# First block's rows by a one-hot product, counts in three products and block stores on ScalarE's DMA queue, in the experts of two layers

## What is computed

```python
def moe(x, router_w, router_b, w_gate, w_up, w_down):
    scores = sigmoid(xf @ router_w)
    biased = scores + router_b
    # best group by its two best, then the two best experts of that group
    _, idx = lax.top_k(jnp.where(in_group, biased, -jnp.inf), TOP_K)
    w = take_along_axis(scores, idx); w = w / sum(w)
    counts = jnp.bincount(idx.reshape(NK), length=N_EXPERTS)
    # each expert's rows stand together in buf, in blocks of a fixed number of rows
    buf = zeros.at[dest].set(xf[tok_sorted])
    def expert_block(args):
        xb, e = args
        hb = jax.nn.silu(xb @ w_gate[e]) * (xb @ w_up[e])
        return hb @ w_down[e]
    y = lax.map(expert_block, (buf, block_e))
    return zeros.at[tok_sorted].add(y[dest] * w_sorted[:, None])
```

## Time and profile before

| | |
|---|---|
| median of 3 runs | 3671.52 us (3670.55 to 3679.8) |
| the profiled execution, its own time | 3671.27 us |
| its span, first to last instruction | 3668.9 us |
| PE matmul busy | 3219.1 us, 88% |
| DVE, ACT, POOL busy | 36%, 18%, 10% |
| mean granted TensorE clock | 0.924 |
| share of the 16 DMA engines: SP's queue, POOL's queue | 58.3%, 6.1% |

### The profile page before, as it was taken

One profiled execution on the slowest core, in us unless ns is written; L12 is line 12 of the kernel. 1 busy time (PEld: TensorE's weight loads), 2 busy tenths in 40 slices (PEclk: granted clock), 3 DMA queues, 4 the chain that ended last, 5 costly groups with the idle time before them and its releaser, 6 DMA issues. The chain is left out here.

```text
span 3668.9 us, 42417 instructions
## 1 busy us (share of the span) xinstructions
PE 3219.1 (88%) x16213; PEld 1599.3 (44%) x16213; DVE 1308.1 (36%) x2932; ACT 664.4 (18%) x1378; POOL 371.2 (10%) x462
## 2 busy tenths in 40 slices
PE   8988599939967799629999999888699999999998
PEld 5454344414544344314444444565434443444344
DVE  6442111133253111054999951274412122212222
ACT  1142122121321122120010021253101010101011
POOL 0122111130001111221000000024100000000000
PEclk9989799969978899859999999999799999999999
DMA  7861899732012999525333442792489999999995
GB/s 262 244 224 59 299 360 343 272 101 65 0 45 87 337 366 348 187 98 184 103 103 134 116 166 103 262 323 74 190 334 412 417 406 406 411 417 406 405 414 205
DMA packets 282493, 888.49 MB, mean 242 GB/s; under 512 B 35744, under 2 KB 75008, under 8 KB 233232
## 3 DMA queue, kind: packets, MB, share of 16 engines
q1 hardware_dynamic: 253200, 807.56, 58.3%
q0 software_dynamic: 29184, 79.48, 6.1%
HBM read 805.93 MB, written 80.99 MB: 242 GB/s over the span
## 5 line engine op out<-in xcount | busy, mean ns | idle before, releaser
L2813 PE MATMUL ec_gu<-ec_ring,ec_xg 128*64 128x512 f32 x2048 | 454.6, 595 | 0.9 <-ACT ec_xg L2965 0.9
L245 PE MATMUL proj_ps<-xT,proj_w 128*128 128x512 f32 x992 | 430.4, 596 | 0.0
L245 PE MATMUL proj_ps<-proj_w,xT 128*128 128x512 f32 (+2 forms) x896 | 359.4, 564 | 18.9 <-DMA proj_w<-in_w_in 18.9
L245 PEld LDWEIGHTS proj_ps<-xT,proj_w 128*128 128x128 f32 x992 | 189.2, 191 | 237.3 <-issue 236.8
L2813 PEld LDWEIGHTS ec_gu<-ec_ring,ec_xg 128*64 128x64 f32 x2048 | 142.0, 137 | 303.3 <-issue 303.3
L245 PEld LDWEIGHTS proj_ps<-proj_w,xT 128*128 128x128 f32 x896 | 171.8, 192 | 204.6 <-issue 155.3
L2842 PE MATMUL ec_yp<-ec_ring,ec_hT 128*64 128x512 f32 x1024 | 247.9, 635 | 0.0
L1130 PE MATMUL moe_gu_ps<-moe_w,moe_xg 128*64 128x512 f32 x1024 | 231.5, 605 | 17.8 <-ACT moe_xg L1245 17.8
L696 PE MATMUL mix_o<-mix_w,xT 128*128 128x512 f32 x384 | 172.0, 608 | 20.3 <-DMA mix_w<-in_w_out 20.3
L274 ACT ACTIVATE proj_o<-proj_ps 128x512 f32<-128x512 f32 (+1 forms) x120 | 70.8, 590 | 611.9 <-PE proj_ps L245 611.9
L1991 DVE SCALAR_TENSOR_TENSOR band_big<-proj_hit,proj_row,band_big 128x516 f32<-128x516 f32 x256 | 173.5, 750 | 2.4
(11 more groups left out here) (504 smaller groups left out, 3711.2 us busy)
## 6 DMA issues: line engine op xcount, KB each, us to landing
ec_ring<-in_w_gate SPq DMA_DIRECT2D x128, 1024.0 KB, 9.3
ec_ring<-in_w_up SPq DMA_DIRECT2D x128, 1024.0 KB, 11.6
ec_ring<-in_w_down SPq DMA_DIRECT2D x128, 1024.0 KB, 12.4
moe_w<-in_exp_w_gate SPq DMA_DIRECT2D x32, 2048.0 KB
moe_w<-in_exp_w_up SPq DMA_DIRECT2D x32, 2048.0 KB
moe_w<-in_exp_w_down SPq DMA_DIRECT2D x32, 2048.0 KB, 10.8
proj_w<-in_w_in SPq DMA_DIRECT2D x22, 2048.0 KB, 10.9
proj_w<-in_w_ada SPq DMA_DIRECT2D x16, 1536.0 KB
```

Of the source, the lines that this page charges most:

```text
L245: mm = nc.tensor.matmul(bank[0:jb["op"], 0:jb["ow"]], lhs, rhs, start=(k == 0), stop=(k == nk - 1))
L2813: mm = nc.tensor.matmul(gu_ps[n][half, :], xg[:, k, c0:c0 + CAP], w[:, m * D_FF + n * 512:m * D_FF + (n + 1) * 512], start=(k == 0), stop= ...
```

## The change

1. **Counts.** `both` is summed over earlier tiles by DVE into `acc` (five small additions and a copy), so that PE needs three products instead of 14. The number of blocks of each expert comes from one comparison with all multiples of 96 (`over`) and one reduction instead of five additions in a row. 
2. **First block by a one-hot product.** DVE builds `oneh` of [128, 4, 96]: 1 where a token's place is row s of block 0. In `moe_experts` PE makes the transposed rows of block 0 as products `x` by `oneh` (`first_x`: 32 products of 128x96, four tiles summed, into banks `x_ps` and `h_ps`). So block 0's rows are not loaded.
3. **The scatter is in `moe_experts`.** POOL issues its 8 indirect DMAs after that stage's barrier. SP issues the three loads of `w[1]`, waits for the scatter (`put`), and then loads block 1's rows.
4. **Stores.** `rows_out` on ScalarE issues two DMAs per block in place of POOL's six, with the halves and quarters as the outer dimension of the DRAM view, [2, 64, 512] and [4, 32, 256]. There are semaphores `stored[r]` for each r; ScalarE waits for the last ones at the end.

```diff
 route:
+        acc, thr, over = st.sb("acc", [P, NT + 1, E]), st.sb("thr", [P, Q]), st.sb("over", [P, E, Q])
-                for t in range(NT):
-                    mm = nc.tensor.matmul(cm[:, NT * E:(NT + 1) * E], ones[:], both[:, t, :], start=(t == 0), stop=(t == NT - 1))
-                for t in range(NT):
-                    for a in range(t):
-                        nc.tensor.matmul(cm[:, t * E:(t + 1) * E], ones[:], both[:, a, :], start=(a == 0), stop=False)
-                    mm = nc.tensor.matmul(cm[:, t * E:(t + 1) * E], strict[:], both[:, t, :], start=(t == 0), stop=True)
-                mm.then_inc(cum_ready, 1)
-            (POOL) pool.wait_ge(idx_ready, 1); 8 x indirect_dma_start(...).then_inc(put, 16); pool.wait_ge(put, 16 * 2 * NT)
+                nc.tensor.matmul(cm[:, 0:NT * E], strict[:], flat(both[:]), start=True, stop=False)
+                nc.tensor.matmul(cm[:, 0:NT * E], ones[:], flat(acc[:, 0:NT, :]), start=False, stop=True)
+                nc.tensor.matmul(cm[:, NT * E:(NT + 1) * E], ones[:], acc[:, NT, :], start=True, stop=True).then_inc(cum_ready, 1)
...
-                V.tensor_add(both[:], oh[0][:], oh[1][:]).then_inc(m_ready, 1)
+                V.tensor_add(both[:], oh[0][:], oh[1][:])
+                V.drain()
+                V.tensor_copy(acc[:, 1, :], both[:, 0, :])
+                V.tensor_add(acc[:, 2, :], both[:, 0, :], both[:, 1, :])
+                V.tensor_add(starts[:], both[:, 2, :], both[:, 3, :])
+                V.drain()
+                V.tensor_add(acc[:, 3, :], acc[:, 2, :], both[:, 2, :])
+                V.tensor_add(acc[:, 4, :], acc[:, 2, :], starts[:])
+                V.drain().then_inc(m_ready, 1)
...
-                for q in range(1, S // MOE_ROWS + 1):
-                    V.scalar_tensor_tensor(nb[:], cnt, float(q * MOE_ROWS), nb[:], ALU.is_gt, ALU.add)
-                    V.drain()
+                V.tensor_tensor(over[:], cnt.unsqueeze(2).to_broadcast([P, E, Q]), thr[:].unsqueeze(1).to_broadcast([P, E, Q]), ALU.is_gt)
+                V.drain()
+                V.tensor_reduce(nb[:], over[:], AX.X, ALU.add)
...
+                V.tensor_tensor(oneh[:], row_no, posA[:].unsqueeze(2).to_broadcast(wide), ALU.is_equal)
+                V.tensor_tensor(at_b[:], row_no, posB[:].unsqueeze(2).to_broadcast(wide), ALU.is_equal)
+                V.drain()
+                V.tensor_add(oneh[:], oneh[:], at_b[:])
 moe_experts, SP:
-                rows(0, 0)
-                rows(1, 1)
                 for n in range(3):
                     moe_load(sp, w[1], w_ready[1], weights, n, second)
+                sp.wait_ge(put, 16 * 2 * NT)
+                rows(1, 1)
 PE:
+                def first_x(h):
+                    bank = (x_ps, h_ps)[h]
+                    for c in range(4):
+                        for t in range(NT):
+                            mm = nc.tensor.matmul(bank[:, c * MB:(c + 1) * MB], x[:, t, (4 * h + c) * P:(4 * h + c + 1) * P],
+                                                  oneh[:, t, :], start=(t == 0), stop=(t == NT - 1))
+                    mm.then_inc(turned, 1)
-                turn_x(0, 0, 0, 0)
-                turn_x(0, 0, 0, 1)
+                first_x(0)
+                first_x(1)
 ScalarE, rows_out:
-                    act.wait_ge(yb_free, b + 1)
+                    act.wait_ge(stored[r], 32 * i + 32)
...
                     nc.scalar.drain().then_inc(y_copied, 1)
+                    act.wait_ge(y_copied, b + 2)
+                    act.dma_start(y_dram[ds(b * MB, MAIN), :].rearrange("s (h n) -> h s n", h=2), yb[r][:]).then_inc(stored[r], 16)
+                    act.dma_start(y_dram[ds(b * MB + MAIN, TAIL), :].rearrange("s (q n) -> q s n", q=4), ytb[r][:]) \
+                        .then_inc(stored[r], 16)
...
+                for r in range(2):
+                    act.wait_ge(stored[r], 32 * n1 + 64)
 POOL:
-                (store: 6 dma_start per block, wait for them, yb_free)
+                (the scatter's 8 indirect_dma_start, moved here from route)
```

More of the change, by code:

```diff
@@ L883, in rms, with route @@
     return dict(kind="rms", eps=EPS2, gain=gain, shift=shift, one_plus=one_plus)
-def route(nc, name, x, escore, router_b, sbr, strict, ones, iota, weights, w0, w0_ready, slots_dram):
+def route(nc, name, escore, router_b, sbr, idx, oneh, strict, ones, iota, weights, w0, w0_ready):
     posA, posB, wA, wB, blk_e = sbr
@@ L896, in route @@
         loaded, m_ready, cum_ready = st.sem("loaded"), st.sem("m_ready"), st.sem("cum_ready")
-        idx_ready, put = st.sem("idx_ready"), st.sem("put")
         cm = st.ps("cm")
@@ L903, in route @@
         g1, wsum = st.sb("g1", [P, NT]), st.sb("wsum", [P, NT])
-        nb, ends, starts, zero = (st.sb(n, [P, E]) for n in ("nb", "ends", "starts", "zero"))
+        nb, ends, starts = (st.sb(n, [P, E]) for n in ("nb", "ends", "starts"))
+        Q = S // MOE_ROWS
+        acc, thr, over = st.sb("acc", [P, NT + 1, E]), st.sb("thr", [P, Q]), st.sb("over", [P, E, Q])
+        at_b = st.sb("at_b", [P, NT, MOE_ROWS])
         below = st.sb("below", [P, B, E])
         bl, nbl = st.sb("bl", [P, B]), st.sb("nbl", [P, 1])
-        idx = [st.sb(f"idx{n}", [P, NT], U32) for n in range(2)]
         flat = lambda v: v.rearrange("p t e -> p (t e)")
@@ L944, in _ @@
                     V.memset(rank_g[:, :, g:g + 1], float(N_GRP - g))
-                V.memset(zero[:], 0.0)
-                V.memset(nb[:], 1.0)
+                V.memset(acc[:, 0, :], 0.0)
+                V.tensor_scalar(thr[:], iota[:, 1:Q + 1], float(MOE_ROWS), None, ALU.mult)
                 V.tensor_scalar(tmp[:], escore[:], 1.0, None, ALU.add)
@@ L1008, in _ @@
                 cnt = cm[:, NT * E:(NT + 1) * E]
-                for q in range(1, S // MOE_ROWS + 1):
-                    V.scalar_tensor_tensor(nb[:], cnt, float(q * MOE_ROWS), nb[:], ALU.is_gt, ALU.add)
-                    V.drain()
-                V.tensor_tensor_scan(ends[:], nb[:], zero[:], 0.0, ALU.add, ALU.add)
+                V.tensor_tensor(over[:], cnt.unsqueeze(2).to_broadcast([P, E, Q]), thr[:].unsqueeze(1).to_broadcast([P, E, Q]),
+                                ALU.is_gt)
                 V.drain()
-                V.tensor_sub(starts[:], ends[:], nb[:])
+                V.tensor_reduce(nb[:], over[:], AX.X, ALU.add)
+                V.drain()
+                V.tensor_tensor_scan(ends[:], nb[:], ones[:, 0:E], 0.0, ALU.add, ALU.add)
+                V.drain()
+                V.scalar_tensor_tensor(starts[:], ends[:], 1.0, nb[:], ALU.subtract, ALU.subtract)
                 V.drain()
@@ L1026, in _ @@
                 V.tensor_copy(idx[1][:], posB[:])
-                V.drain().then_inc(idx_ready, 1)
+                wide = [P, NT, MOE_ROWS]
+                row_no = iota[:, 0:MOE_ROWS].unsqueeze(1).to_broadcast(wide)
+                V.tensor_tensor(oneh[:], row_no, posA[:].unsqueeze(2).to_broadcast(wide), ALU.is_equal)
+                V.tensor_tensor(at_b[:], row_no, posB[:].unsqueeze(2).to_broadcast(wide), ALU.is_equal)
+                V.drain()
+                V.tensor_add(oneh[:], oneh[:], at_b[:])
                 V.tensor_tensor(below[:], iota[:, 0:B].unsqueeze(2).to_broadcast([P, B, E]),
@@ L1045, in moe_load, with moe_experts @@
     sp.dma_start(w[n][:], weights[n][ds(e, 1)].rearrange("a (k p) n -> p (a k) n", p=P)).then_inc(w_ready[n], 16)
-def moe_experts(nc, name, ident, sbr, slots_dram, weights, y_dram, w, w_ready):
+def moe_experts(nc, name, x, ident, sbr, idx, oneh, slots_dram, weights, y_dram, w, w_ready):
     blk_e = sbr[4]
@@ L1077, in moe_experts @@
         down_ready, y_copied = st.sem("down_ready"), st.sem("y_copied")
-        stored, yb_free = st.sem("stored"), st.sem("yb_free")
+        stored, put = [st.sem(f"stored{r}") for r in range(2)], st.sem("put")
         def pairs_less_one(eng):
@@ L1183, in body @@
                     if more:
-                        turn_x(2 * i + 2, 0, i + 1, 0)
+                        turn_x(2 * i + 2, 0, i, 0)
                     down(i, 0)
                     if more:
-                        turn_x(2 * i + 2, 0, i + 1, 1)
+                        turn_x(2 * i + 2, 0, i, 1)
                     turn_h(i, 1)
@@ L1239, in _, with copy_x @@
                 act.sem_inc(y_copied, 1)
-                act.sem_inc(yb_free, 2)
+                for r in range(2):
+                    act.sem_inc(stored[r], 32)
                 n1 = pairs_less_one(act)
-                def copy_x(b, r, h):
+                def copy_x(b, r, h, bank=x_ps):
                     act.wait_ge(turned, 2 * b + h + 2)
-                    nc.scalar.activation(xg[r][:, 4 * h:4 * h + 4, :].rearrange("p c s -> p (c s)"), x_ps[:, 0:4 * MB],
+                    nc.scalar.activation(xg[r][:, 4 * h:4 * h + 4, :].rearrange("p c s -> p (c s)"), bank[:, 0:4 * MB],
                                          ACT.Copy).then_inc(xg_copied, 1)
@@ L1279, in _ @@
                 copy_x(0, 0, 0)
-                copy_x(0, 0, 1)
```

(15 more changed lines are left out.)

## The result

| | before | after |
|---|---|---|
| median | 3672.89 us | 3759.7 us (3758.87 to 3768.16) |
| ratio | | 1.0238, 95% interval 1.0218 to 1.0259 |
| span | 3668.9 us | 3757.8 us |
| mean granted clock | 0.924 | 0.918 |

Slower by 87 us, where +96 (41 to 157) was forecast as 3767 (3712 to 3828). First the stretches of the changed kernel: the loop, then the end of the stage, when only the last block's two stores are in flight.

What follows compares the result with a forecast made beforehand. PE was taken to bound the expert loop, with the DMA engines just below. From 3671.3 us, the loop's +102, the end's -6 and the start's 0 gave 3767 us, range 3712 to 3828.

Steps and rivals of the forecast that it cites:

- The bound and the loop: Expert loop: stores load engines 0 and 1 beyond PE's 40.1 us per pair; PE waits for weights, +51 us per layer.
- the middle: Loop: weights fall behind 7.2 to 11.4 us per pair; the forecast took 9.3, between engine rates of 24.6 and 22.6 GB/s.
- The 14 us: Loop: time to spare between a weight load's arrival and its use, subtracted once per layer from 65 us of delay.
- ScalarE's issue: Loop: ScalarE issues stores ahead of its copy of the next rows; claimed no added time, as PE would await weights.
- The sign to look for: Loop: PE waiting for `moe_w` in most pairs from the third on, mainly before `gate_up`, would show the forecast right.
- The end: Last result copy to next stage: POOL's 7.9 us drain hidden, last store on two engines; -3 us per layer (-4 to 0).
- The rival's -8.8: End of stage: stores spread over all 16 engines would land the last one earlier, gaining 8.8 us per layer; chance 0.09.
- The start: Counts to block 1's `gate_up`: earlier start spent waiting for block 1's rows; 0 us per layer (-4 to +4).
- Worth 10 us: Start of the layer: the gain claimed for the early start if block 1's rows did not stand last in the queue.
- (a): Rival on the stores: they spread over all 16 engines, the loop stays PE's, 3654 us in all; chance 0.09.
- (b): Rival on the stores: few engines but other ones each time, only the end gains 3 us per layer, 3665 us; chance 0.04.
- one twin in the trace: Line L2193's load with DRAM view [4, 32, 1024]: DMA share 0.26, 104 GB/s, taken as 4 of 16 engines.

Runs made afterwards that it cites:

- the six pieces: The changed kernel with its two stores per block cut into six (two for `yb`, four for `ytb`), still issued by ScalarE: 3668.3 us, 0.9974 of the kernel before.
- `ytb` alone: The changed kernel with `yb` stored in two halves over 16 engines and only `ytb` as one DMA on four engines: 3669.9 us, 0.9986 of the kernel before.
- late issue: The changed kernel, same stores and queue, the second block's store issued behind the next pair's first activations: 3743.3 us, 1.0189 of the kernel before.
- both blocks as products: The changed kernel with six-piece stores on ScalarE and block 1's rows also made by a one-hot product: 3650.9 us, 0.9941 of the kernel before.

## Why the prediction was right

- **The bound and the loop.** PE's loop runs just above the DMA engines, and what decides is the most loaded engine. Right: the six pieces take the loss away, `ytb` alone costs nothing, late issue shows the waits and periods of the forecast. The size was 51 for 42.3 us. The mis-sized term is the period, 49.4 forecast, 46.85 measured over the first six, at 1164 / 46.85 = 24.8 GB/s per engine, close to the 24.6 that I had as the best and passed over for the middle. (It was not the best: 104 / 4 = 26 GB/s stands in rows 5.) The 14 us that I took off again were in fact not to be had; the two errors partly cancel. That the sum came within 7 us of the median is luck in part: the loops were 17 us shorter than forecast in both layers, the starts and the untouched later stages some 11 us longer.
- **ScalarE's issue.** "Where the queue is full ScalarE stands for microseconds, but PE is then waiting for weights. Nothing is added" is the step that failed. PE waited for ScalarE and never for weights, and 16 us of the loss hang on it. The sign to look for, waits for `moe_w`, did not appear; read by that alone, the right forecast would have looked refuted.
- **The end.** POOL's 7.9 us and the two-engine store: -3 for -3.3. The rival's -8.8 was measured as -8.7.
- **The start.** Counts and block numbers came as worked out: DVE goes on at 386.24 (386.3), `idx` is cast at 388.53 (388.9), the last step starts at 392.38. PE waited 14.2 us for block 1's rows (6 to 13 forecast); they came at 426.69, then `turn_x` and the larger part of the tail ran at half clock (0.90 and 5.49 us for 0.55 and 3.66): 0.6 + 0.35 + 1.8 = +2.8, inside -4 to +4. "Worth 10 us" without the rows at the end of the queue is reached with both blocks as products (49.8 to 40.2 us, 9.6); asking for the rows earlier gave 5.9.
- **The rivals.** (a) and (b) are out on ScalarE's queue; what (b) supposed, other engines each time, fits POOL's. That they could be excluded rested on one twin in the trace, `band_big<-dv`.

## What to carry to other kernels

Merging DMAs into one view saves issues, but on ScalarE's and SP's queues here the outer dimension of the DRAM side set how many engines carried it; look in the trace for a twin of the view and read the DMA share while it is alone. Then sum the bytes of the most loaded engine, loads included, and compare with the period, and ask who stands behind an issue that can't return. When two causes lie on each other, the wait in the profile names the one that comes last, not the one that is left when it is removed.

## What the hardware showed beyond that

- ScalarE's issue stood for 5.3 to 8.7 us with 98 to 108 packets of `yb` per engine still to start, though SP's queue takes 128 per engine without a stand (two weight loads, issued in 0.4 and 0.6 us). The count at which an issue goes on is no constant of these runs.
- POOL's queue took the same views without loss, at a DMA share of 0.28 where ScalarE's gave 0.20, and up to 6.5 engines at work where ScalarE's had 4.05. Which engines they are is not in the trace.
- In a loop where PE is 95% busy and waits for no transfer the granted clock fell in two to six of seven pairs, 1.7 us each (a pair is 39.4 or 41.1 us), in the cases that I looked at just after PE had run its small transposes of `hid` and waited 0.7 us for DVE. A gain of 5 us at the start was given back in this way. Why one layer has two such pairs and another six stays open; with both blocks as products the same kernel had six in the first layer and two in the second.
